# A bias row on TensorE: one float32 row at the head of a block, or two float32r rows of a padded tile in its middle

## What is computed

```python
proj = jnp.einsum('bsd,dc->bsc', rmsnorm(x, norm_g), w_in)
gates = jax.nn.sigmoid(proj[..., QKVG_COLS + N_HEADS:] + b_gate).reshape(b, s, N_BRANCH, D_MODEL)
...
up = jnp.einsum('bsnw,nwd->bsnd', ys, w_up)      # ys: outputs of the three attention branches
merged = jnp.sum(gates * up, axis=2)
```

## Time and profile before

| | |
|---|---|
| median of three runs | 2377.92 us |
| the profiled execution, by its own time | 2372.76 us |
| its span, first to last instruction | 2371.0 us |
| TensorE busy | 2266.2 us, 96% |
| DVE busy | 1533.2 us, 65% |
| ACT busy | 1042.9 us, 44% |
| mean granted TensorE clock | 0.982 |
| blocks 12 to 15, with the adds | 372 to 487 us of the span |
| the eight pairs | 511 to 758 us of the span |

### The profile page before, as it was taken

How to read it: one execution, slowest core, us unless ns; L and a number is a source line. 1 busy time by engine, 2 the same in 40 slices (tenths; PEclk the granted TensorE clock), 3 DMA queues, 4 the chain that set the end, 5 groups by cost and what they waited for, 6 DMA issues and landing times.

```text
span 2371.0 us, 29865 instructions
## 1 busy us (share of the span) xinstructions
PE 2266.2 (96%) x10504; PEld 1806.5 (76%) x10504; DVE 1533.2 (65%) x2177; ACT 1042.9 (44%) x1304; POOL 48.2 (2%) x94
## 2 busy tenths in 40 slices
PE   6999999999999999999999999898999999989997
PEld 5677777777777787876787777677888888877886
DVE  5355567756565878773554778656777877774444
ACT  4333445543333434347433443434555555554442
POOL 0000000000001000000000000000000000000000
PEclk9999999999999999999999999999999999999999
DMA  7777777867677879773433332464556556565663
GB/s 242 249 273 265 253 259 265 275 221 255 220 256 233 312 242 347 276 266 107 133 107 124 90 89 89 138 195 160 187 176 195 179 186 195 174 215 174 195 194 128
DMA packets 279232, 482.39 MB, mean 203 GB/s; under 512 B 21530, under 2 KB 112780, under 8 KB 276952
## 3 DMA queue, kind: packets, MB, share of 16 engines
q1 hardware_dynamic: 274440, 464.85, 60.0%
q0 software_dynamic: 4688, 16.15, 2.0%
HBM read 474.46 MB, written 6.46 MB: 203 GB/s over the span
## 4 chain that ended last, share of the span: by engine, by line
PE 77%; DVE 8%; ACT 6%; issue 5%; DMA 3%; SPq 0%; DVEq 0%; ACTq 0%; POOL 0%; POOLq 0%
PE gemm_ps L1510 66%; ACT w_hi L569 3%; DVE w_lo L906 2%; DMA mraw<-in_w_mod_dram 2%; DVE tmpT L937 1%; PE ps L1537 1%; PE ps L1881 1%; PE gemm_ps L1525 1%; PE ps L1934 1%; PE ps L2018 1%; PE ps L1941 1%; DVE msum L1039 1%; DMA w_raw<-in_w_down_dram 1%; PE ps L1886 0%; DVE sc L1375 0%
## 5 line engine op out<-in xcount | busy, mean ns | idle before, releaser
L906 DVE TENSOR_TENSOR w_lo<-w_raw,w_hi 128x1024 fp32r<-128x1024 f32 x688 | 833.1, 1222 | 568.0 <-ACT w_hi L569 562.1
L1510 PE MATMUL gemm_ps<-w_hi,a_hi 128*128 128x512 f32 (+1 forms) x2304 | 943.0, 409 | 21.9 <-DVE a_lo L944 16.7
L569 ACT ACTIVATE w_hi<-w_raw 128x1024 fp32r<-128x1024 f32 x688 | 713.4, 1054 | 506.1 <-PE gemm_ps L1510 427.9
L1510 PE MATMUL gemm_ps<-w_lo,a_hi 128*128 128x512 f32 (+1 forms) x2304 | 904.2, 392 | 0.0
L1510 PE MATMUL gemm_ps<-w_hi,a_lo 128*128 128x512 f32 (+1 forms) x2304 | 904.1, 392 | 0.0
L1510 PEld LDWEIGHTS gemm_ps<-w_hi,a_hi 128*128 128x128 f32 x2304 | 438.7, 190 | 162.1 <-issue 50.4
L1510 PEld LDWEIGHTS gemm_ps<-w_hi,a_lo 128*128 128x128 f32 x2304 | 438.4, 190 | 94.2
L1510 PEld LDWEIGHTS gemm_ps<-w_lo,a_hi 128*128 128x128 f32 x2304 | 439.2, 191 | 92.1 <-issue 8.9
L1429 DVE SCALAR_TENSOR_TENSOR acc<-gp,cw,acc 128x256 f32<-128x256 f32 x344 | 151.5, 480 | 13.8 <-DVE acc L1429 1.4
L1039 DVE SCALAR_TENSOR_TENSOR msum<-mraw,cs,msum 128x1024 f32<-128x1024 f32 x120 | 153.3, 1278 | 0.4
L1510 PE MATMUL gemm_ps<-w_hi,ft_hi 128*128 128x512 f32 x344 | 135.7, 394 | 3.1 <-DVE w_lo L906 3.1
(11 more groups left out here) (351 smaller groups left out, 1576.7 us busy)
## 6 DMA issues: line engine op xcount, KB each, us to landing
w_raw<-in_w_in_dram SPq DMA_DIRECT2D x336, 512.0 KB, 4.4
mraw<-in_w_mod_dram SPq DMA_DIRECT2D x192, 512.0 KB, 5.9
w_raw<-in_w_up_dram SPq DMA_DIRECT2D x336, 256.0 KB, 3.0
w_raw<-in_w_down_dram SPq DMA_DIRECT2D x84, 512.0 KB, 4.2
w_raw<-in_w_out_dram SPq DMA_DIRECT2D x64, 512.0 KB, 4.2
w_raw<-in_w_up_dram SPq DMA_DIRECT2D x24, 512.0 KB, 4.9
x_d<-xres POOLq DMA_DIRECT2D x2, 2048.0 KB, 7.9
x_sb<-in_x_dram SPq DMA_DIRECT2D x2, 1024.0 KB, 5.9
```

The costliest lines, as they stand in the source:

```text
L569: act.activation(w_hi[:, slot], raw[:, slot], ACT.Copy).then_inc(hi_done, 1)
L906: dve.tensor_tensor(w_lo[:, slot], raw[:, slot], w_hi[:, slot].bitcast(F32), ALU.subtract).then_inc(lo_done, 1)
L1510: mm = pe.matmul(gemm_ps[:, bank, rt, 0:n], x[:, chunk0 + k, tok], w[:, slot, kk, 0:n], start=(k == 0 and part == 0 and not opened), stop= ...
```

## The change

The row of 512 is brought to two partitions of a new tile bsrc. ACT and DVE turn it into the first two rows of a 128-partition float32r tile brow, whose other rows are zeroed once: ACT writes bsrc times a scale of +1 on partition 0 and -1 on partition 1, rounded to float32r (plus and minus the high part); DVE adds 0 times bsrc on partition 0 and 1 times bsrc on partition 1 (the high part stays; the low part comes out). TensorE multiplies a 128x128 tile of ones with it, one float32r matmul per token tile, after unit 4 of the block and without start; the product opens its bank itself. ACT does its step at the head of the block, ahead of the split of unit 2, after it has seen the row's transfer (brow_in) and that TensorE has finished unit 5 of the gate block before; DVE does its own after ACT's (brow_hi), also ahead of unit 2; SP fetches the next row after DVE's step (brow_set). The constants (ones, zeros, and the two scales) are set by DVE in block 3.

```diff
--- before.py
+++ after.py
@@ -225,7 +225,9 @@
     br = [at(f"br{i}", [P, RT, 4 * BW], F32, 129.5 + 16 * i) for i in range(2)]
     ys_hi = at("ys_hi", [P, NBR * HEADS, T], F32R, 161.5)
     ys_lo = at("ys_lo", [P, NBR * HEADS, T], F32R, 173.5)
-    brow = at("brow", [1, NBLK], F32, 185.5)
+    bsrc = at("bsrc", [2, NBLK], F32, 185.5)
+    brow = at("brow", [P, NBLK], F32R, 187.5)
+    ones = at("ones", [P, P], F32R, 204)
     relb = at("relb", [P, HEADS, T], F32, 189.5)
     msum = at("msum", [P, 2, NBLK], F32, 189.5)
     tmpT = at("tmpT", [P, 2, UK, T], F32, 193.5)
@@ -327,7 +329,7 @@
         return sems[name]
 
     raw_in = [S(f"raw_in{i}") for i in range(SLOTS)]
-    brow_in = S("brow_in")
+    brow_in, brow_hi, brow_set = S("brow_in"), S("brow_hi"), S("brow_set")
     mod_in = [S(f"mod_in{i}") for i in range(SLOTS)]
     mod_used, mod_evac, mod_out = S("mod_used"), S("mod_evac"), S("mod_out")
     sum_used, sum_fold = S("sum_used"), S("sum_fold")
@@ -422,8 +424,8 @@
             bg = a["b_gate"]
             for g in range(DC):
                 if g:
-                    sp.wait_ge(used, U_GATE0 + BU * (g - 1) + 1)
-                sp.dma_start(brow[:, :], bg[:, g * NBLK:(g + 1) * NBLK]).then_inc(brow_in, 16)
+                    sp.wait_ge(brow_set, g)
+                sp.dma_start(bsrc[:, :], bg[0, g * NBLK:(g + 1) * NBLK].partition_broadcast(2)).then_inc(brow_in, 16)
                 b = 12 + g
                 units(w_in, 2 * b, GATE0 + g * NBLK, mod=fetches(b))
             for c in range(DC):
@@ -434,8 +436,8 @@
                     c = 2 * n + c2
                     for j in range(2):
 
-                        sp.wait_ge(used, U_PAIRS + 2 * PAIR * c + (1 if j else 1 - PAIR))
-                        sp.dma_start(brow[:, :], bg[:, bass.ds((j + 1) * D + c * NBLK, NBLK)]).then_inc(brow_in, 16)
+                        sp.wait_ge(brow_set, DC + 2 * c + j)
+                        sp.dma_start(bsrc[:, :], bg[0, bass.ds((j + 1) * D + c * NBLK, NBLK)].partition_broadcast(2)).then_inc(brow_in, 16)
                         q = U_PAIRS // SLOTS + 2 * PAIR // SLOTS * c
 
                         def row_of_pair(first):
@@ -628,9 +630,18 @@
                     me(act.activation(fl[:, 3:5, 0:HEADS], fl[:, 3:5, 0:HEADS], ACT.Exp, scale=-1.0))
                     act.activation(fl[:, 3:5, 0:HEADS], fl[:, 3:5, 0:HEADS], ACT.Ln, bias=1.0).then_inc(S("f_sp"), 1)
 
+            def bias_row(n, row_used):
+
+                act.wait_ge(S("ones_set"), 1)
+                act.wait_ge(brow_in, 16 * (n + 1))
+                act.wait_ge(used, row_used)
+                act.activation(brow[0:2, :], bsrc[:, :], ACT.Identity, scale=stat[0:2, 46:47]).then_inc(brow_hi, 1)
+
             for seg in range(4):
                 for b in range(4):
                     B = 4 * seg + b
+                    if seg == 3:
+                        bias_row(b, U_GATE0 + BU * (b - 1) + 6)
                     for i in range(2, 10):
 
                         if B == 0:
@@ -651,6 +662,7 @@
             with act.Fori(0, DC) as c:
                 q = U_PAIRS // SLOTS + 2 * PAIR // SLOTS * c
                 for j in range(2):
+                    bias_row(DC + 2 * c + j, U_PAIRS + 2 * PAIR * c + (6 if j else 6 - PAIR))
                     splits(q, PAIR * j + 2, PAIR * j + BU + 2)
                     act.wait_ge(used, U_PAIRS + 2 * PAIR * c + PAIR * j + BU)
                     act.wait_ge(evac_dve, DC + 2 * c + j)
@@ -1071,7 +1083,17 @@
             diagonals()
             splits(0, 0, 2)
 
+            def bias_row(n):
+
+                dve.wait_ge(brow_hi, n + 1)
+                dve.scalar_tensor_tensor(out=brow[0:2, :], in0=bsrc[:, :], scalar=ident[0:2, 1:2], in1=brow[0:2, :].bitcast(F32),
+                                         op0=ALU.mult, op1=ALU.add).then_inc(brow_set, 1)
+
             def forget_gates(B, i):
+                if (B, i) == (3, 8):
+                    dve.memset(ones[:, :].bitcast(F32), 1.0)
+                    dve.memset(brow[:, :].bitcast(F32), 0.0)
+                    dve.tensor_tensor(stat[0:2, 46:47], ident[0:2, 0:1], ident[0:2, 1:2], ALU.subtract).then_inc(S("ones_set"), 1)
                 if (B, i) == (2, 3):
                     dve.wait_ge(S("f_parts"), 1)
                     dve.tensor_copy(fparts[:, :], pC[:, 0:T]).then_inc(S("f_copied"), 1)
@@ -1090,6 +1112,8 @@
             for seg in range(4):
                 for b in range(4):
                     B = 4 * seg + b
+                    if seg == 3:
+                        bias_row(b)
                     for i in range(2, 10):
                         if B == 0:
                             turned("x", i - 2, vec[:, 0:16])
@@ -1113,6 +1137,7 @@
                     c = 2 * n + c2
                     q = U_PAIRS // SLOTS + 2 * PAIR // SLOTS * c
                     for j in range(2):
+                        bias_row(DC + 2 * c + j)
                         for i in range(2, PAIR + 2):
                             splits(q, PAIR * j + i, PAIR * j + i + 1)
                             at_unit = 2 * PAIR * c2 + PAIR * j + i
@@ -1484,7 +1509,7 @@
 
         @block.tensor
         def _(pe):
-            def product(u0, slot0, bank, hi, lo, units, chunk0=0, opened=False, after=None, chunks=None, n=NBLK,
+            def product(u0, slot0, bank, hi, lo, units, chunk0=0, after=None, chunks=None, n=NBLK,
                         halfway=None, turning=None, turned=None,
                         turning_next=None):
 
@@ -1508,7 +1533,7 @@
                             tok = slice(rt * P, (rt + 1) * P)
                             for part, (x, w) in enumerate(((hi, w_hi), (hi, w_lo), (lo, w_hi))):
                                 mm = pe.matmul(gemm_ps[:, bank, rt, 0:n], x[:, chunk0 + k, tok], w[:, slot, kk, 0:n],
-                                               start=(k == 0 and part == 0 and not opened),
+                                               start=(k == 0 and part == 0),
                                                stop=(k == chunks - 1 and part == 2))
                         if halfway and kk == 0:
                             halfway(i)
@@ -1520,9 +1545,11 @@
                     if after:
                         after(i)
 
-            def add_row(bank):
+            def add_row(n, bank):
+
+                pe.wait_ge(brow_set, n + 1)
                 for rt in range(RT):
-                    pe.matmul(gemm_ps[:, bank, rt], C("sel", 1, 0, P), brow[:, :], start=True, stop=False)
+                    pe.matmul(gemm_ps[:, bank, rt], ones[:, :], brow[:, :], start=False, stop=False)
 
             def mod_group(m, half):
 
@@ -1687,17 +1714,16 @@
                     B = 4 * seg + b
                     if B >= 2:
                         pe.wait_ge(evac_act, B - 1)
-                    if seg == 3:
-                        pe.wait_ge(brow_in, 16 * (b + 1))
-                        add_row(B % 2)
 
                     def after(u):
                         if seg:
                             head(seg - 1, b, u)
                         else:
                             forget_gates(B, u)
+                        if seg == 3 and u == 4:
+                            add_row(b, B % 2)
                         modulation(B, u)
-                    product(BU * B, 0, B % 2, a_hi, a_lo, BU, opened=(seg == 3), after=after,
+                    product(BU * B, 0, B % 2, a_hi, a_lo, BU, after=after,
                             turning=("x", x_sb, True, 0) if B == 0 else None)
             pe.wait_ge(S("h_ylo"), NBR * HEADS)
             for c in range(DC):
@@ -1713,11 +1739,14 @@
                     c = 2 * n + c2
                     for j in range(2):
                         u0 = U_PAIRS + 2 * PAIR * c + PAIR * j
-                        pe.wait_ge(brow_in, 16 * (DC + 2 * c + j + 1))
                         pe.wait_ge(evac_act, 16 + 2 * c + j)
-                        add_row(0)
-                        product(u0, PAIR * j, 0, a_hi, a_lo, BU, opened=True,
-                                after=lambda u: sum_over_partitions(PAIR_SUMS[0] + n) if (c2, j, u) == (1, 1, 6) else None)
+
+                        def after(u):
+                            if u == 4:
+                                add_row(DC + 2 * c + j, 0)
+                            if (c2, j, u) == (1, 1, 6):
+                                sum_over_partitions(PAIR_SUMS[0] + n)
+                        product(u0, PAIR * j, 0, a_hi, a_lo, BU, after=after)
                         pe.wait_ge(evac_dve, DC + 2 * c + j)
                         product(u0 + BU, PAIR * j + BU, 1, ys_hi, ys_lo, UPU, chunk0=4 * (j + 1))
             pe.wait_ge(evac_dve, 12)
```

## The result

The median went from 2381.49 us (four runs, 2377.76 to 2387.09) to 2344.77 us (2344.15 to 2349.36). The medians are 36.7 us apart; the ratio of the runs is 0.9867, interval 0.9847 to 0.9888, which is 31.7 us, between 26.7 and 36.4. The forecast was 29.1 us less, and 2348.8 us in a range of 2338 to 2362. The changed kernel was run again later beside other ones and gave a ratio of 0.9878 (0.9858 to 0.9897) with a median of 2349.9, some 29 us. The profiled executions differ by 28.4 us in their spans, 2371.0 and 2342.6.

A forecast was written before the change was run, and what follows sets the result against it. TensorE's own queue was taken to bound the kernel. Pairs (13.1 and 9.7 of clock) and gate blocks (6.3) sum to 29.1 us off a median of 2377.9, giving 2348.8 us, range 2338 to 2362.

The forecast's parts named there:

- The old add, 2.10 us in a dense block: At a dense block's head, the one-row float32 bias add costs TensorE 2.10 us.
- The new add, 0.46 us: After unit 4, two 128x128 on 128x512 float32r matmuls cost 0.46 us, as the product matmuls around them do.
- The half clock, 7 x 1.62: Between 370 and 755 us, all seven half-clock stretches go with the one-row matmuls, 1.62 us each.
- Theory A: In the blocks with adds, matmuls using few array rows let the clock fall; padding alone gains 7 x 1.62 = 11.3 us.
- The first rival: Clock falls at block borders stay, or ones and zeros count as little as one row: 2358.5 us; chance 0.12.
- The seventh, in block 14: The one half-clock stretch outside the pairs, in block 14, goes too, gaining 1.62 us.
- The hand-over at the head of a block: ACT's new step takes 0.72 us, DVE's 0.68; unit 2 stalls 0.4, 2.0, 0.4 us in blocks 13 to 15.
- The gate blocks, 6.3 us: Blocks 12 to 15 gain 6.3 us: 2.1 in 12, 1.25 each in 13 and 15, 1.7 in 14.
- The pairs, 22.8 us: The eight pairs gain 8 x 1.64 = 13.1 us from the add and 6 x 1.6 = 9.7 of clock.
- second rival: ACT's Identity costs table loads, 1.28 us each in blocks 13 to 15, giving 3.8 back: 2352.6 us; chance 0.04.
- The third and fourth rivals: Unit 2 comes late in each pair, 2371.2 us, chance 0.06; SP's row wait stalls block transfers, 2429 us, chance 0.04.
- The thin cover of 0.8 us: In the pairs, unit 2's w_lo is ready 0.8 us before TensorE wants it, so no stall.

## Why the prediction was right, point by point

**The old add, 2.10 us in a dense block.** Nearly right in size, wrong in the reason for a part of it. The plain step is 27.20 / 120 = 0.227 us and not 0.229, because the 27.43 us that I divided had 0.2 of the add's price in them; so the old add cost 1.91 + 27.43 - 27.20 = 2.14. I put 0.19 of it down to the float32 form. With 128 rows in float32, 0.37 us are gone, and with two rows in float32r 0.42 are there: they belong to the change of the number of rows.

**The new add, 0.46 us.** 0.45 in the chain. Zeros and ones cost what the products beside them cost.

**The half clock, 7 x 1.62.** This was the step with the most in it for the least evidence, and it held: all six in the pairs are gone, in both executions of the changed kernel. Theory A was tested in two ways that don't depend on each other, the float32 row padded at its old place, and 2 against 128 rows at the new one. The Trainium skill ("TensorE: Matmul & The Clock Gate", Part 1) has the clock gate follow how busy TensorE is; in the pairs here it fell with TensorE busy throughout (27.30 us of 27.30 ahead of one fall), behind matmuls with one or two rows, and behind adds with 128 rows it never did. So TensorE's busy time alone doesn't tell whether the clock holds; the rows of its matmuls bear on it too. The first rival fell with that.

**The seventh, in block 14.** I had warned that the new wait of 2 us could keep it, and counted its 1.62 us as gained even so. It was there in one of two executions of the changed kernel, 1.6 us, behind the wait and no longer behind an add.

**The hand-over at the head of a block.** ACT's step was put at 0.72 and is 0.706; DVE's at 0.68 and is 0.733. The waits at unit 2 in blocks 13 to 15 were put at 0.4, 2.0 and 0.4 and came to 0.5, 2.0 and 0.5 (3.0 in three). They cost more than they last. From the first transpose behind unit 1 to the first score it is 3.40 us in block 12, without a wait, and 4.14 in block 13, 0.74 more for a wait of 0.5:

```profile
376.64 0.38 PE L1637 MATMUL ps<-cst,br 128*128 128x128 f32 x2
...
380.04 0.59 PE L1665 MATMUL ps<-qkgT 128*128 128x256 f32 x2
...
402.60 0.38 PE L1637 MATMUL ps<-cst,br 128*128 128x128 f32 x2
...
406.74 0.59 PE L1665 MATMUL ps<-qkgT 128*128 128x256 f32 x2
```

Block 14 loses 2.33 in the execution in which its clock stays up, block 15 0.75: 3.8 us in all where the sum had 2.8. In the pairs there was none, as forecast. What I missed is how the gate blocks hang together: with the add gone, the chain between the blocks runs along DVE's sums and yT. I had found the room of unit 2 correctly from its own rows without seeing that DVE, not ACT, sets the start of it. At the end of block 13, ACT stands 8.39 us waiting for yT, and goes to its table load at 427.81 right behind the step that needed it; DVE has begun its backlog at 421.95, behind TensorE's sum over partitions:

```profile
427.38 0.42 ACT L611 ACTIVATE ys_hi<-yT 128x256 fp32r<-128x256 f32 x1 [8.39 <-DVE yT L1025]
```

```profile
421.95 0.68 DVE L1058 COPY mrow<-ps 64x512 f32<-64x512 f32 x1 [4.66 <-PE ps L1573]
```

**The gate blocks, 6.3 us.** 3.9 in one execution and 5.5 in the other. The half-clock stretch is 1.6 of the missing 2.4, the waits at unit 2 took 1.0 more than I gave them, and the four adds, at 2.14 - 0.45 = 1.69 each in place of 1.64, gave 0.2 back. In the second execution the clock's 1.6 is not missing, and the other two make the 0.8 that is. The wait before L1650, in which I let the new add hide, did take it up: TensorE's own 1.1 us of waiting there are gone from the list of waits.

**The pairs, 22.8 us.** 22.9. Each pair is 27.65 us where I said 27.9, again because the price of going over and back was hidden in the 27.43.

**The table loads (second rival).** None was added: in the pairs ACT has no table load at all, as before, and in the gate blocks they are the same ones. Identity runs beside the sigmoid; that agrees with the Trainium skill ("ScalarE: Activation LUTs", Table sets).

**The third and fourth rivals.** The thin cover of 0.8 us in the pairs held, and SP's new wait cost nothing: no wait of TensorE for w_lo or for the row is left in the pairs.

The sum was 29.1; the profiled spans say 28.4, the two series of runs 32 and 29. That the spans come so near is luck in part: in the stretches of the sum it was 26.8, and the 1.6 us that lie outside them happened to fall on the right side. The forecast of the median, 2348.8, started from a median of three runs; the fourth run of the kernel before put that 3.6 us higher.

## What to carry to other kernels

In this kernel a matmul with one or two rows in a dense float32r stream cost more than its own time: some 0.4 us for going over and back, and, where such matmuls lasted some 2 us, a half-clock stretch worth 1.6 us behind about every second add. Padding with zeros to 128 rows cost TensorE nothing (0.45 us for two matmuls, the price of any two of this stream); it takes room in all 128 partitions and one memset. Ask of every bias or mask row in a dense stream whether it could have 128. And when something is taken out of a block's head, look at which preparation ran beside it: here the room to the next limit was only some 2.3 us, the change used it up, and turning two steps round won 3 to 5 us back. Measure such a second step in its own stretch, since the rest of the kernel scatters by as much.

## What the runs showed that was not expected

- The switch between few-row and 128-row matmuls costs 0.37 us (float32, one row) and 0.42 us (float32r, two rows) per add, about half at each end.
- The same kernel with the same 2.0 us wait had a half-clock stretch behind it in one execution and not in another.
- Whole runs of one kernel differ by several us (2345.6 to 2352.9 in one series), which is more than the re-ordering of the gate blocks is worth. The half-clock stretches move about from one profiled execution to the next, but they don't explain this scatter alone: behind the pairs the two executions of the changed kernel have the same 54.6 us at half clock (without the last 20 us of the span), and took 1612.4 and 1616.4 us there. The cause stays open.
